# Moving the four weight sums of the Strassen pairs from VectorE to GpSimd in a two-layer decoder step

## What is computed

```python
def _swiglu(x, ln, w_in, w_out):
    h = _rms(x, ln) @ w_in
    a, b = h[..., :D_FF], h[..., D_FF:]
    return (jax.nn.silu(a) * b) @ w_out

x = x + _swiglu(x, ln_ffn[layer], w_ffn_in[layer], w_ffn_out[layer])
```

## Time and profile before

| | |
|---|---|
| median of 3 runs | 1604.82 us (1603.63 to 1604.85) |
| the profiled execution | 1602.77 us |
| its span, first to last instruction | 1601.0 us |
| TensorE busy | 1525.3 us |
| VectorE busy | 948.5 us |
| ScalarE busy | 552.2 us |
| GpSimd busy | 123.3 us |

### The profile page before, as it was taken

How to read it: one execution, slowest core, us unless ns; L and a number is a source line. 1 busy time by engine, 2 the same in 40 slices (tenths; PEclk the granted TensorE clock), 3 DMA queues, 4 the chain that set the end, 5 groups by cost and what they waited for, 6 DMA issues and landing times.

```text
span 1601.0 us, 27546 instructions
## 1 busy us (share of the span) xinstructions
PE 1525.3 (95%) x11425; PEld 1429.5 (89%) x11425; DVE 948.5 (59%) x1284; ACT 552.2 (34%) x851; POOL 123.3 (8%) x111
## 2 busy tenths in 40 slices
PE   7999999999999889999999999988788999999997
PEld 7779978978987789999999999887688999999997
DVE  6547437436634787637736767564558754763663
ACT  5233133123223353313422345453446232332331
POOL 0000001001000110000000021341221000000001
PEclk9999999999999999999999999998898999999999
DMA  6346217216323323132222232111112213223223
GB/s 235 113 169 211 94 66 255 93 60 222 127 73 125 110 82 105 53 105 105 79 83 102 79 136 80 62 41 54 40 40 79 105 66 117 80 79 119 69 76 108
DMA packets 50149, 164.00 MB, mean 102 GB/s; under 512 B 5264, under 2 KB 6608, under 8 KB 50032
## 3 DMA queue, kind: packets, MB, share of 16 engines
q1 hardware_dynamic: 41888, 134.56, 24.6%
q0 software_dynamic: 6416, 24.93, 4.3%
q10 hardware_dynamic: 1760, 3.31, 0.6%
HBM read 141.35 MB, written 23.46 MB: 103 GB/s over the span
## 4 chain that ended last, share of the span: by engine, by line
PE 83%; DVE 8%; ACT 3%; issue 3%; POOL 1%; DMA 1%; ACTq 0%; DVEq 0%; POOLq 0%
PE ps L462 48%; PE ps L1119 13%; PE ps L476 8%; PE ps L1302 3%; DVE arena L1392 3%; PE ps L976 2%; PE ps L985 1%; DVE w_lo L450 1%; PE ps L1007 1%; PE ps L993 1%; PE ps L1293 1%; PE ps L1265 1%; ACT w_hi L445 1%; DVE rstd L511 1%; PE ps L963 1%
## 5 line engine op out<-in xcount | busy, mean ns | idle before, releaser
L445 ACT ACTIVATE w_hi<-w_raw 128x1024 fp32r<-128x1024 f32 x180 | 188.6, 1055 | 366.8 <-PE ps L462 203.6
L462 PE MATMUL ps<-xg_hi,w_hi 128*128 128x272 f32 x1280 | 269.2, 292 | 19.8 <-DVE xg_lo L1398 7.8
L462 PE MATMUL ps<-xg_hi,w_lo 128*128 128x272 f32 x1280 | 266.1, 289 | 0.0
L462 PE MATMUL ps<-xg_lo,w_hi 128*128 128x272 f32 x1280 | 265.5, 289 | 0.0
L450 DVE TENSOR_TENSOR w_lo<-w_raw,w_hi 128x1024 fp32r<-128x1024 f32 x172 | 212.8, 1241 | 74.2 <-ACT w_hi L445 70.0
L462 PEld LDWEIGHTS ps<-xg_hi,w_hi 128*128 128x128 f32 x1280 | 203.9, 190 | 29.7 <-issue 12.7
L462 PE MATMUL ps<-pr_hi,w_hi 128*128 128x272 f32 x992 | 211.0, 292 | 11.5 <-DVE pr_lo L1392 4.5
L462 PE MATMUL ps<-pr_hi,w_lo 128*128 128x272 f32 x992 | 209.9, 291 | 0.0
L462 PE MATMUL ps<-pr_lo,w_hi 128*128 128x272 f32 x992 | 209.4, 290 | 0.0
L462 PEld LDWEIGHTS ps<-xg_lo,w_hi 128*128 128x128 f32 x1280 | 202.5, 190 | 0.0
L462 PEld LDWEIGHTS ps<-xg_hi,w_lo 128*128 128x128 f32 x1280 | 201.3, 190 | 0.0
(11 more groups left out here) (247 smaller groups left out, 2632.1 us busy)
## 6 DMA issues: line engine op xcount, KB each, us to landing
w_raw<-in_w SPq DMA_DIRECT2D x180, 512.0 KB, 3.4
arena<-in_w SPq DMA_DIRECT2D x40, 512.0 KB, 4.0
arena<-in_state SPq DMA_DIRECT2D x32, 512.0 KB, 4.9
out_st_s<-arena POOLq DMA_DIRECT2D x32, 512.0 KB, 4.1
x<-in_x ACTq DMA_DIRECT2D x4, 544.0 KB, 6.0
out_y<-x POOLq DMA_DIRECT2D x8, 272.0 KB, 2.3
out_st_p<-arena SPq DMA_DIRECT2D x4, 512.0 KB, 2.8
arena<-in_dec POOLq DMA_DIRECT2D x4, 256.0 KB, 3.0
```

The source lines that it names most:

```text
L445: nc.scalar.activation(w_hi[:, n.c % 4, :], w_raw[:, n.c % 2, :], ACT.Copy).then_inc(w_hi_done, 1)
L462: last = pe.matmul(ps[:, 2 * bank_pair + s, 0:HT], w_of(w, k), xm[:, k, s * HT:(s + 1) * HT], start=(k == 0 and w == 0 and xi == 0), stop= ...
```

## The change

The four sums of each pair are taken out of VectorE's program and put into GpSimd's: `all_sums(layer)` stands after the sums of squares that precede the layer's feed-forward, and ahead of GpSimd's next table loads (layer 0) or output transfers (layer 1). It waits for `tlo_done`, then for each of the ten pairs for the splits of the pair before (`w_lo_done`) and the two loads, and makes s1, s3, s2, s4 with waits for s1 and s2 on a semaphore of its own. VectorE's turn loses its call of `sums`, and its chain counter goes from 5 to 3 a turn. ScalarE, TensorE and SyncE are unchanged.

```diff
+            s2, s4, s3, s1 = (s_sum[:, z, :] for z in range(4))
+            a11, a12, a21, a22 = (s_raw[:, z // 2, 512 * (z % 2):512 * (z % 2) + 512] for z in range(4))
+
+            def sums(n, s):
+
+                gp.wait_ge(w_lo_done, n.v)
+                for c in range(2):
+                    gp.wait_ge(sr_in[c], (s + 1).times(16).v)
+                nc.gpsimd.tensor_tensor(s1, a21, a22, ALU.add).then_inc(sum_chain, 1)
+                nc.gpsimd.tensor_tensor(s3, a11, a21, ALU.subtract)
+                gp.wait_ge(sum_chain, (s.times(2) + 1).v)
+                nc.gpsimd.tensor_tensor(s2, s1, a11, ALU.subtract).then_inc(sum_chain, 1)
+                gp.wait_ge(sum_chain, (s.times(2) + 2).v)
+                nc.gpsimd.tensor_tensor(s4, a12, s2, ALU.subtract).then_inc(sums_done, 1)
+
+            def all_sums(layer):
+                gp.wait_ge(tlo_done, 2 * (layer + 1))
+                for b, turns in mixed_turns(layer):
+                    with gp.Fori(0, turns) as i:
+                        sums(Index(b).loop(4, i), Index(mixed_before(b)).loop(1, i))
...
             for k in range(1, KT):
                 sumsq(1, k)
+            all_sums(0)
...
             for k in range(1, KT):
                 sumsq(3, k)
+            all_sums(1)
...
-                def sums(s):
-                    for c in range(2):
-                        dve.wait_ge(sr_in[c], (s + 1).times(16).v)
-                    ch.link(tt(s1, a21, a22, ALU.add))
-                    tt(s3, a11, a21, ALU.subtract)
-                    ch.link(tt(s2, s1, a11, ALU.subtract))
-                    tt(s4, a12, s2, ALU.subtract).then_inc(sums_done, 1)
...
                     dve.wait_ge(evac, (n + (3 + BIAS - N_FFN0)).v)
-                    if more:
-                        sums(s + 1)
                     dve.wait_ge(st_mm, (s.times(3) + 3).v)
...
-                    sums(Index(s0))
```

More of the change, by code:

```diff
@@ L245, in build @@
         stat_mm, stat_sqrt, rstd_done = sem("stat_mm"), sem("stat_sqrt"), sem("rstd_done")
-        sq_ready, gp_chain, v_chain, a_chain = sem("sq_ready"), sem("gp_chain"), sem("v_chain"), sem("a_chain")
+        sum_chain, sq_ready, gp_chain, v_chain, a_chain = sem("sum_chain"), sem("sq_ready"), sem("gp_chain"), sem("v_chain"), sem("a_chain")
         x_in, x_squared, dec_in = [sem(f"x_in{k}") for k in range(KT // 2)], sem("x_squared"), sem("dec_in")
@@ L1645, in first_turn, with mixed_turn @@
                         hidden_lo(q, m, p2)
-                s2, s4, s3, s1 = (s_sum[:, z, :] for z in range(4))
-                a11, a12, a21, a22 = (s_raw[:, z // 2, 512 * (z % 2):512 * (z % 2) + 512] for z in range(4))
-                def sums(s):
-                    for c in range(2):
-                        dve.wait_ge(sr_in[c], (s + 1).times(16).v)
-                    ch.link(tt(s1, a21, a22, ALU.add))
-                    tt(s3, a11, a21, ALU.subtract)
-                    ch.link(tt(s2, s1, a11, ALU.subtract))
-                    tt(s4, a12, s2, ALU.subtract).then_inc(sums_done, 1)
-                def mixed_turn(n, q, m, s, more):
+                a22 = s_raw[:, 1, 512:1024]
+                def mixed_turn(n, q, m, s):
                     dve.wait_ge(st_hi, (s.times(3) + 1).v)
@@ L1698, in ffn @@
                     s0 = mixed_before(b)
-                    sums(Index(s0))
                     with dve.Fori(0, turns - 1) as i:
[L1701 to L1704, removed]
+                        ch.enter(i, 3)
+                        mixed_turn(Index(b).loop(4, i), Index(pairs + 2 * first).loop(2, i), Index(2 * first).loop(2, i), Index(s0).loop(1, i))
+                        ch.leave(turns - 1, 3)
+                    mixed_turn(Index(b + 4 * (turns - 1)), Index(pairs + np_ - 2), Index(np_ - 2), Index(s0 + turns - 1))
                     n0, pairs = n0 + 2 * np_, pairs + np_
```

## The result

The changed kernel takes 1611.94 us (median of five runs, 1610.98 to 1613.54) against 1604.82 us (also the median of five, 1603.12 to 1605.99); the ratio is 1.0048, with a 95% interval from 1.0033 to 1.0063. It is slower, by 5.3 to 10.1 us.

The account below looks back on a forecast made before the run. TensorE, busy 95% of the span and without pause in the mixed turns, bounds the kernel. 0 + 0 + 6.3 us takes the profiled 1602.77 to 1609.1; as a median, 2.05 us higher, 1611.1 us, range 1604.2 to 1614.5.

Parts of the forecast that it names:

- the two waits: TensorE's waits for `out_a` before each layer's first mixed turn: to grow from 5.6 and 3.5 to about 8.5 and 6.9 us.
- What is removed: 80 sums, 55 us, leave VectorE; off the path, since TensorE never pauses in a turn, so 0 gained.
- One sum, 1.27 us: Time of one 128x512 addition on GpSimd, scaled from its 128x544 adds, with 1.04 and 1.35 us as ends.
- Turns are taken: A VectorE instruction with two SBUF operands waits for at most one sum, and a sum for at most one such instruction.
- The first turn, 2.9 + 3.4 us: First pair's sums delay VectorE's chain to `out_a`, which TensorE waits for: 2.9 us in layer 0, 3.4 in layer 1.
- about 0.2 us later: In each layer's first turn, GpSimd's first sum starts this long after the loads' traffic ends, at 590.8 and 1225.9.
- rival (a): Not slower: sums start late or spaced out and miss VectorE's first-turn chain; 1604.8 to 1606.7 us, chance 0.22.
- The prediction's own rules: Turns taken in the first turn; a blocked 0.73 us instruction ends 0.55 us after release, a 1.18 us split 1.07 us after.
- The slower restart, 0: After its wait TensorE runs 3.3 us at a granted clock of 0.53; a longer wait should add nothing.
- Ordinary turns, 0: In ordinary turns VectorE's evacuation comes up to 2.5 us late, within 5.1 us of cover, so no cost.

Follow-up runs that it names:

- late first pair: The changed kernel with GpSimd's sums of each layer held until VectorE's second `out_a` of the first turn; 1606.93 us, ratio 1.0005 to the kernel before.
- idle additions: The kernel before, sums on VectorE, plus four unneeded GpSimd additions beside the first turn of each layer; 1611.81 us, ratio 1.0035.
- two early sums: The changed kernel with each layer's first pair held between s3 and s2 until VectorE's second `out_a`; 1608.98 us, ratio 1.0022 to the kernel before.
- memsets: The kernel before, sums on VectorE, plus eight GpSimd memsets of 544 columns beside each layer's first turn; 1604.56 us, ratio 0.9997.
- copies: The kernel before, sums on VectorE, plus eight GpSimd copies of 512 columns beside each layer's first turn; 1609.56 us, ratio 1.0022.
- twice the work: The changed kernel, first pair's sums held until the second `out_a`, plus four unneeded GpSimd additions behind every pair's sums; 1607.12 us, ratio 1.0007 to the kernel before.

## Why the prediction was right, and where its steps were not

**Direction, place and size.** 1611.1 us was forecast and 1611.94 measured, and the two waits were named. The late first pair and the idle additions show the place from both sides: take the collision away and the loss is gone, put it alone into the kernel before and most of the loss is there (ratio 1.0035 beside 1.0048, with overlapping intervals).

**What is removed: 0.** Right. TensorE has no wait inside the turns before or after, and with the collision taken away no gain is left that the runs can tell.

**One sum, 1.27 us.** Right: 1.27 and 1.28 us where it runs alone. The figure scaled from the Trainium skill's GPSIMD Engine Reference (section 3.1), an estimate of 1.12 us, is 0.15 us short of that.

**Turns are taken.** Right: in the changed kernel each held VectorE instruction waits for one sum, and with two sums in place of four half of the delay is left.

**The first turn, 2.9 + 3.4 us.** This step had the right mechanism and the wrong size, mainly by one term: the start "about 0.2 us later" than the landing. It was 1.0 and 0.7 us; rival (a) had named just this gap as shown nowhere. So `multiply` went ahead, s4 came behind the splits, and three sums stood in the chain in place of four. The prediction's own rules, with `multiply` first, give 2.4 us a layer. The rest is the sums: one that was held ended 1.13 us after its release, not about 1.25. Measured were 2.09 + 2.08 us, so the waits are 7.7 and 5.5 us and not 8.5 and 6.9.

**The slower restart, 0.** This "smaller term" failed: "a longer wait should add nothing". With it the first blocks took 1.26 and 0.61 us more, and the idle additions repeat that (14.98 and 14.42 us for the two first blocks). The errors, about 2.1 us too much and 1.9 us too little, cancel, and the sum of 6.3 meets the 6.0 us that the feed-forwards lost. The forecast's closeness owes that much to chance.

**Ordinary turns, 0.** Right: the evacuation was late in five turns of the 20, by 1.4 us at most where up to 2.5 was reckoned, and TensorE did not wait. In six turns, the last of each round, no sum runs at all. The remainder of the 7.1 us between the medians, 1.1 us, lies inside the interval.

## What to carry to other kernels

An engine that is idle for most of a stage is no free place: here a GpSimd operation that reads SBUF and a VectorE instruction with two SBUF operands held each other up where they met, the later one standing still until the first was through. So ask what VectorE is doing at the moment the operation is released, above all where TensorE waits for VectorE. "As soon as the data have landed" was the wrong release for a result that is needed only later; here one more wait removed the whole loss. And where the engine that sets the time has no wait inside a loop, work taken from another engine in that loop buys nothing: look for the waits at its edges, and shorten the chain that ends them.

## What the hardware showed that was not expected

GpSimd's first instruction after a load that it waits for starts some time after the traffic has ended: 1.0 us in layer 0 of the changed kernel (593.0 to 593.99), and about 0.6 to 0.8 us in its layer 1 and in both layers of the runs with two early sums and with idle additions, memsets and copies.

The low clock after a wait of TensorE does not follow the length of the wait. First blocks of 13.69 to 13.76 us came after waits of 5.6 and 3.5 us (before); 14.95 and 14.37 after 7.7 and 5.5 us (the change); but 15.00 after 4.2 us in layer 1 of the run with the copies, and 14.19 after 5.6 us in layer 0 of the late first pair. Within a layer there is an order: the eight first blocks behind a chain that GpSimd held (the change, idle additions, copies, two early sums) took 14.37 to 15.00 us, and the eight behind a chain that it did not hold (before, late first pair, memsets, twice the work) 13.69 to 14.19. Why a longer wait comes with a longer low clock, and not in proportion, stays open; for a sum it is a term between 0 and 1.3 us for each such wait.
